# Work of the heads' stretch and after it is split in advance, kept in DRAM and loaded back; heads unrolled, sigmoids moved

## The reference, cut to what matters

```python
mod = silu_c @ ada_w[l] + ada_b[l]                  # shifts, scales, gates from c
h = _modulate(_rmsnorm(x, norm_w[l, 0]), sh1, sc1)
# layer 0, per head: one projection h @ w_in split in q, v, z_fwd, z_bwd, g; then
f = lb + (1.0 - lb) * jax.nn.sigmoid(z)             # k = (1 - lb) * sigmoid(-z)
S_t = diag(f_t) S_{t-1} + k_t v_t^T                 # both directions, o_t = S_t^T q_t
y = (rmsnorm(o_f + o_b) * g_norm * silu(g)) @ w_out
# layer 1: y = (gate_b * conv3(gate_c * xin)) @ w_out
x = x + g1 * _rmsnorm(y, norm_w[l, 1])
hf = _modulate(_rmsnorm(x, norm_w[l, 2]), sh2, sc2)
x = x + g2 * _rmsnorm((silu(gate) * up) @ ffn_w_out, norm_w[l, 3])
```

## Time and profile before

| | |
|---|---|
| time, median of 3 runs | 2781.76 us (2780.82 to 2784.55) |
| profiled execution: time, span | 2777.81 us, 2776.1 us |
| mean clock of PE granted over the span | 0.984 |
| busy: PE, PE's weight loads, DVE, ACT, POOL | 95%, 79%, 61%, 35%, 42% |
| transfers | 202.06 MB, mean 73 GB/s |
| chain that ended last | PE 75%, DVE 12%, issue 5%, ACT 3%, POOL 3%, DMA 1% |

### The profile page before, as it was taken

The page is one execution under the profiler, slowest core; times in us unless marked ns, Lnnn a source line. Parts: engine busy times, 40 slices in busy tenths (PEclk is TensorE's granted clock), DMA queues, the critical chain, the costliest instruction groups (busy, mean ns, idle before and its releaser), DMA issues.

```text
span 2776.1 us, 37193 instructions
## 1 busy us (share of the span) xinstructions
PE 2630.0 (95%) x12824; PEld 2183.6 (79%) x12824; DVE 1695.3 (61%) x2380; ACT 960.0 (35%) x1853; POOL 1165.1 (42%) x799
## 2 busy tenths in 40 slices
PE   7999999999969789999999989999897999999998
PEld 5788888888858668888888877888686888888886
DVE  6277668766875575656565565665438555554556
ACT  5334433443443642332223254111254233222323
POOL 2111111111160086665556542444517666556662
PEclk9999999999989999999999999999999999999999
DMA  6111221111110312122112132333311112111113
GB/s 244 61 46 39 62 62 46 40 61 54 39 53 13 133 39 75 62 82 77 60 60 69 60 137 91 118 117 114 129 61 38 61 46 68 53 45 45 60 46 144
DMA packets 57899, 202.06 MB, mean 73 GB/s; under 512 B 6832, under 2 KB 6832, under 8 KB 57776
## 3 DMA queue, kind: packets, MB, share of 16 engines
q1 hardware_dynamic: 57776, 200.41, 21.5%
HBM read 183.61 MB, written 16.78 MB: 72 GB/s over the span
## 4 chain that ended last, share of the span: by engine, by line
PE 75%; DVE 12%; issue 5%; ACT 3%; POOL 3%; DMA 1%; SPq 0%; DVEq 0%; POOLq 0%; ACTq 0%
PE psum L1027 16%; PE psum L1029 15%; PE psum L1028 15%; PE psum L1546 5%; PE psum L1548 5%; PE psum L1547 5%; PE psum L1222 2%; PE psum L1267 2%; PE psum L1269 2%; PE psum L1268 2%; DVE q_all L2431 1%; DVE c_set L2228 1%; PE psum L1236 1%; DVE q_all L2525 1%; DVE k_all L2424 1%
## 5 line engine op out<-in xcount | busy, mean ns | idle before, releaser
L1027 PE MATMUL psum<-x_hi,unit_hi 128*128 128x512 f32 x1232 | 486.9, 395 | 20.8 <-DVE x_lo L2228 12.8
L1028 PE MATMUL psum<-x_lo,unit_hi 128*128 128x512 f32 x1232 | 483.1, 392 | 0.0
L1029 PE MATMUL psum<-x_hi,unit_lo 128*128 128x512 f32 x1232 | 482.7, 392 | 0.0
L902 POOL TENSOR_TENSOR unit_sum<-ffn_raw 128x512 f32<-128x512 f32 x220 | 298.2, 1355 | 416.4 <-PE psum L1027 182.3
L2228 DVE TENSOR_TENSOR c_set<-c_set,psum 128x512 f32<-128x512 f32 x352 | 233.3, 685 | 345.8 <-PE psum L1029 179.7
L907 POOL TENSOR_TENSOR unit_lo<-unit_sum,unit_hi 128x512 fp32r<-128x512 f32 x220 | 286.8, 1312 | 185.1 <-ACT unit_hi L1660 184.9
L857 POOL TENSOR_TENSOR w_lo<-w_raw,w_hi 128x1024 fp32r<-128x1024 f32 x38 | 94.2, 2479 | 626.8 <-ACT w_hi L1660 626.8
L1027 PEld LDWEIGHTS psum<-x_hi,unit_hi 128*128 128x128 f32 x1232 | 233.3, 189 | 79.4 <-issue 22.6
L2228 DVE TENSOR_TENSOR y<-y,psum 128x512 f32<-128x512 f32 x288 | 193.7, 686 | 159.1 <-PE psum L1548 154.7
L1027 PE MATMUL psum<-h_hi,w_hi 128*128 128x512 f32 x640 | 270.7, 423 | 7.2 <-POOL w_lo L857 4.0
L1029 PEld LDWEIGHTS psum<-x_hi,unit_lo 128*128 128x128 f32 x1232 | 233.4, 189 | 49.4
(11 more groups left out here) (283 smaller groups left out, 5170.8 us busy)
## 6 DMA issues: line engine op xcount, KB each, us to landing
ffn_raw<-in_w_ffn_in SPq DMA_DIRECT2D x88, 512.0 KB, 3.7
ffn_raw<-in_w_ffn_out SPq DMA_DIRECT2D x44, 512.0 KB, 4.0
w_raw<-in_w_hgrn_in SPq DMA_DIRECT2D x40, 512.0 KB, 3.7
ada_raw<-in_ada SPq DMA_DIRECT2D x32, 512.0 KB, 4.3
conv_ada_raw<-in_ada SPq DMA_DIRECT2D x32, 512.0 KB, 4.0
conv_w_raw<-in_w_conv_in SPq DMA_DIRECT2D x24, 512.0 KB, 4.5
ada_first<-in_ada SPq DMA_DIRECT2D x4, 2048.0 KB, 14.8
kept<-xt SPq DMA_DIRECT2D x16, 512.0 KB, 2.8
```

Of the source, the lines that this page charges most:

```text
L902: pool.tensor_tensor(unit[2][:, :], one, other, op).then_inc(S["unit_summed"], 1)
L1027: begin = pe.matmul(out_ap, hi[:, a:b], rhs_hi, start=first, stop=False)
L1028: pe.matmul(out_ap, hi[:, a:b], rhs_lo, start=False, stop=False)
L1029: return begin, pe.matmul(out_ap, lo[:, a:b], rhs_hi, start=False, stop=last)
```

## The change

- New tensors in DRAM: `rows_kept`, `units_kept`, `mix_kept`. In head h (phase 1 to 7) there are three spots in ScalarE's, GpSimd's and SP's programs: A behind the last scores (ScalarE) and before the low part of panel 4 (GpSimd); B behind panel 4's high and low; C behind the last context evacuation (ScalarE), and directly behind B (GpSimd).
- Phases 1 to 3 split four rows each (two at A, two at C): rows 0 to 6 of the first out-projection, rows 3 to 7 of the convolution's. Phases 4 to 7 split the seven units of one FFN pair each (three at A with one sum, two at B and two at C with two sums each). From phase 2 on the mixed output of head phase - 2 is split at B. Each is stored in DRAM.
- They are loaded back where they are used, high and low parts together: rows 0 to 6 and six mixed outputs around the fill, 14 units for each FFN, five convolution rows. The work that made them there is gone. Row 7 and the mixed outputs of the last two heads are split late as before.
- The heads are unrolled on all engines. The sigmoids of a head run at the end of its projection head, before the last evacuation. `panel_high(1)` stands at the start of a head, `merge_level(3)` one evacuation earlier. In the last head ScalarE's order and PE's slots between the v transposes change.
- In the start panel 2 of head 0 has a place of its own and is split early; ScalarE builds four diagonal matrices, with `start_rows(1)` between them; PE does 12 small products first.

```diff
+SPLIT_HGRN, SPLIT_CONV = KB - 1, 3
+SPLIT_ROWS = [(0, r) for r in range(SPLIT_HGRN)] + [(1, r) for r in range(SPLIT_CONV, KB)]
+ROW_PHASES = len(SPLIT_ROWS) // 4
+SPOTS = A_SPOT, B_SPOT, C_SPOT = range(3)
+SPOT_UNITS = (0, 1, 2), (3, 4), (5, 6)
+SPLIT_KINDS = (M2, M4, M3, M5, M1, M7, M6)
+SPLIT_SUMS = tuple(kind for kind in SPLIT_KINDS if kind in SUMMED)
+SPLIT_MIXES = HEADS - 2
+
+
+def row_tasks(phase, spot):
+
+    first = 4 * (phase - 1) + {A_SPOT: 0, C_SPOT: 2}.get(spot, 4)
+    return [t for t in (first, first + 1) if spot != B_SPOT and 1 <= phase <= ROW_PHASES]
+
+
+def split_pair(phase):
+
+    return phase - 1 - ROW_PHASES if phase > ROW_PHASES else None
+
+
+def unit_tasks(phase, spot):
+
+    return [] if split_pair(phase) is None else list(SPOT_UNITS[spot])
...
+    rows_kept = nc.dram_tensor("rows_kept", (len(SPLIT_ROWS), P, 2 * D), F32, kind="Internal").ap()
+    units_kept = nc.dram_tensor("units_kept", (4 * PRODUCTS, P, D), F32, kind="Internal").ap()
+    mix_kept = nc.dram_tensor("mix_kept", (SPLIT_MIXES, 4, P, HALF), F32, kind="Internal").ap()
...
+            def stage_stores(phase, spot):
+
+                for t in row_tasks(phase, spot):
+                    sp.wait_ge(S["stage_low"], t + 1)
+                    sp.dma_start(rows_kept[t], as_f32(stage_row[t % 2][0][:, :, :])).then_inc(S[f"stage_stored{t % 2}"], 16)
+                m = split_mix(phase, spot)
+                if m is not None:
+                    sp.wait_ge(S["mix_split"], m + 1)
+                    for part, tile in enumerate((mix_hi, mix_lo[m % 2])):
+                        sp.dma_start(mix_kept[m, part::2].rearrange("h p t -> p h t"),
+                                     as_f32(tile[:, :]).rearrange("p (h t) -> p h t", h=2)).then_inc(S["mix_stored"], 16)
+                for j in unit_tasks(phase, spot):
+                    pair = split_pair(phase)
+                    sp.wait_ge(S["stage_low"], unit_number(pair, j))
+                    sp.dma_start(units_kept[PRODUCTS * pair + SPLIT_KINDS[j]], as_f32(stage_unit[j % 3][0][:, :, :])
+                                 ).then_inc(S[f"stage_stored{j % 3}"], 16)
...
+            for h in range(HEADS):
+                head_loads(h, h % 2)
...
+            def unit_load(f, k):
+
+                u, kind = FIRST_ORDER[k]
+                if k >= 4:
+                    sp.wait_ge(S["unit_started"], FFN_UNITS * f + k - 2)
+                sp.dma_start(as_f32(unit_parts[k % 4][0][:, :, :]), units_kept[PRODUCTS * (2 * f + u) + kind]
+                             ).then_inc(S[f"unit_loaded{k % 4}"], 16)
...
+            for m in range(SPLIT_MIXES):
+                for part in range(2):
+                    sp.dma_start(as_f32(mix_halves[0][part][0][:, m, :]), mix_kept[m, part]
+                                 ).then_inc(S[f"mix_loaded{m}"], 16)
+                if m == 3:
+                    row_load(4)
...
+            sp.wait_ge(S["gemm_full"], O_END)
+            for r in range(SPLIT_CONV, KB):
+                sp.dma_start(as_f32(conv_row_parts[r][0][:, :, :]), rows_kept[SPLIT_ROWS.index((1, r))]
+                             ).then_inc(S[f"conv_row_loaded{r}"], 16)
...
+            def stage_lows(phase, spot):
+
+                for t in row_tasks(phase, spot):
+                    _, hi, lo, raw = stage_row[t % 2]
+                    pool.wait_ge(S["stage_hi"], t + 1)
+                    pool.tensor_tensor(lo[:, :], raw[:, :], hi[:, :], ALU.subtract).then_inc(S["stage_low"], 1)
+                m = split_mix(phase, spot)
+                if m is not None:
+                    pool.wait_ge(S["mix_hi"], m + 1)
+                    pool.tensor_tensor(mix_lo[m % 2][:, :], mix[m % 2][:, :], mix_hi[:, :], ALU.subtract
                                        ).then_inc(S["mix_split"], 1)
-
-
-            def row_low(r):
-
-                pool.wait_ge(S["w_hi_done"], N_HGRN_OUT + r + 1)
-                pool.tensor_tensor(hgrn_rows[r][1][:, :], row_raws[r][:, :], hgrn_rows[r][0][:, :], ALU.subtract
-                                   ).then_inc(S["panel_split"], 1)
...
+            for n in range(4, N_HGRN_OUT):
+                h, i = n // HEAD_PANELS, n % HEAD_PANELS
+                if i == 4:
+                    stage_spot(h, A_SPOT)
+                panel_low(n, n % 2, ring[n % 2])
+                if i == 4:
+                    stage_spot(h, B_SPOT)
+                    stage_spot(h, C_SPOT)
...
+            for _ in range(12):
+                pe.matmul(bank(2, 0, P), ident[:, :], ident[:, :], start=True, stop=True)
...
+                    slots(6)
                     for part in range(3):
                         v_transposes(hs, part)
-                    slots(28)
+                        slots(1)
+                    slots(19)
                     for part in range(2):
...
+            def stage_highs(phase, spot):
+
+                for t in row_tasks(phase, spot):
+                    act.wait_ge(S[f"stage_loaded{t % 2}"], row_stored(t))
+                    copy(stage_row[t % 2][1], stage_row[t % 2][3][:, :], "stage_hi")
+                m = split_mix(phase, spot)
...
+                def sigmoids():
+
+                    act.wait_ge(S["gemm_evac"], hg * 10 + (4 + O_HEADS + 4))
+                    act.wait_ge(S["ctx_evac"], hg * 3 + 3)
+                    act.wait_ge(S["scan_full"], hg * SCAN_USES + U_TURN)
                     for d in (FWD, BWD):
                         copy(gates[d][:, :], z[d][:, :], "sigmoids", ACT.Sigmoid)
                     for d in (FWD, BWD):
                         copy(k[d][:, :], z[d][:, :], "sigmoids", ACT.Sigmoid, scale=-1.0)
...
+                    copy(first_third[0][:, :], w_raws[0][:, 0, :], "w_hi_done")
...
                 if hg is not None and hs is not None:
                     evacuate(0, 0, cols(z[FWD], 0, CTX))
-                    panel_high(1)
                     evacuate(0, 1, cols(z[FWD], 1, CTX))
                     evacuate_ctx(0, z[FWD][:, 0:CTX])
                     near_copies()
                     evacuate(1, 0, cols(z[BWD], 0, CTX))
                     panel_high(2)
+                    merge_level(3)
                     evacuate(1, 1, cols(z[BWD], 1, CTX))
                     evacuate_ctx(1, z[BWD][:, 0:CTX])
-                    merge_level(3)
                     merge_level(4)
...
                     if not last:
                         panel_high(5)
+                    sigmoids()
...
+                if inst == 0 and i < 4:
+                    return
```

More of the change, by code:

```diff
@@ L99, with split_mix, unit_number, sums_after @@
 PARTIALS = 16 * (FFN_GROUPS - 1)
+SPLIT_HGRN, SPLIT_CONV = KB - 1, 3
[13 more added lines that the diff above has]
+    return [] if split_pair(phase) is None else list(SPOT_UNITS[spot])
+def split_mix(phase, spot):
+    return phase - 2 if spot == B_SPOT and phase >= 2 else None
+def unit_number(pair, j):
+    return len(SPLIT_ROWS) + PRODUCTS * pair + j + 1
+def sums_after(pair, j):
+    return len(SPLIT_SUMS) * pair + sum(kind in SUMMED for kind in SPLIT_KINDS[:j + 1])
+def row_stored(t):
+    return 16 * (t // 2 + 1)
+def unit_stored(pair, j):
+    rows, each = (len(SPLIT_ROWS) // 2, len(SPLIT_ROWS) // 2, 0)[j % 3], (3, 2, 2)[j % 3]
+    return 16 * (rows + each * pair + j // 3 + 1)
 CTX_Q = 4
@@ L336, in build_trunk @@
     ffn_raw = at("ffn_raw", 176, [P, 3, D])
-    units = [unit_at(f"unit{i}", 188 + 4 * i) for i in range(4)]
+    unit_parts = [both_parts(f"unit{i}", 188 + 4 * i, HALF) for i in range(4)]
+    units = [(*parts[1:], at(f"unit{i}_sum", 190 + 4 * i, [P, HALF])) for i, parts in enumerate(unit_parts)]
     last_units = [[unit_at(f"last_unit{f}_{i}", (0, 32)[f] + 4 * i) for i in range(4)] for f in range(2)]
@@ L888, in _, with stage_sums @@
-            mix_low(0, (6,))
-            mix_low(1, range(KB - 1))
-            row_low(7)
+            panel_low(N_HEADS + 2, 0, first_third)
+            panel_low(N_HEADS + 3, 1, ring[1])
+            def stage_sums(phase, spot):
+                pair = split_pair(phase)
+                for j in unit_tasks(phase, spot):
+                    if SPLIT_KINDS[j] not in SUMMED:
+                        continue
+                    if pair == j == 0:
+                        pool.wait_ge(S["stage_stored1"], row_stored(len(SPLIT_ROWS) - 1))
+                    elif pair + j // 3 > 0:
+                        pool.wait_ge(S[f"stage_stored{j % 3}"], unit_stored(pair, j) - 16)
+                    for t in range(2):
+                        pool.wait_ge(S[f"stage_loaded{t}"], row_stored(len(SPLIT_ROWS) - 1) + 16 * (pair + 1))
+                    one, other, op = stage_terms(SPLIT_KINDS[j])
+                    pool.tensor_tensor(stage_unit[j % 3][3][:, :], one, other, op).then_inc(S["stage_sum"], 1)
@@ new lines, in stage_spot @@
+            def stage_spot(phase, spot):
+                stage_sums(phase, spot)
+                stage_lows(phase, spot)
+            for n in range(4, N_HGRN_OUT):
[6 more added lines that the diff above has]
```

(16 more changed lines are left out.)

378 lines of the change are left out of this document (206 added, 172 removed).

## The result

Median 2749.78 us (2748.13 to 2752.59, 4 runs) against 2781.62 us (2780.82 to 2784.55): a ratio of 0.9883, 95% interval 0.9871 to 0.9896, 31.8 us faster. Forecast were 2764, 17.9 faster: the sign and the range hold, the size was too small; the time lies at the lower edge of the forecast's own range (2750 to 2778), between it and rival (b), 2739. The profiled execution took 2749.15, its span 2747.4, so the two spans differ by 28.7; 3 of the 31.8 lie in how the profiled execution of before stood to its median.

The account below looks back on a forecast made before the run. PE was taken as the bound, busy 2630 of 2776 us, idle 146. Terms -2.5 -14 +48.6 -16 -11 -9 -14 = -17.9 gave 2764 from 2781.8; own range 2750 to 2778, 8-in-10 range 2708 to 2786.

Parts of the forecast that it names:

- rival (b): Heads: half of the collisions of VectorE with GpSimd's new work reach PE, 24.3 off, 2739 us; chance .15.
- the last scan: Last head: units ready from DRAM free VectorE from standing behind GpSimd, so near products start earlier, -16 us (-12 to -20).
- projection and FFN 0: First units load instead of being summed and split, so waits for unit lows go: -11 us (-8 to -15).
- conv rows: Convolution rows: five PE waits of 7.4 for GpSimd's lows and one half-clock stretch go, -9 us.
- FFN 1: Second FFN: PE's waits for x's low parts shrink as GpSimd's units are gone there, -14 us (-9 to -17).
- Start: First panels: own place for panel 2 saves 4.0 and clock 1.7, ScalarE's copies cost 3.2; net -2.5 us (-7 to +1).
- The heads' gains: Heads: earlier sigmoids -11, unrolling -3 for two loop turns, merge moved ahead 0; together -14 us.
- The heads' price: Heads: new GpSimd work delays VectorE's ada steps, hence states and PE, with clock loss; +48.6 us (0 to 105).
- knife edge: Heads, spot A: if the last ada step gets in before the panel's low, a unit phase costs 1.2, no clock.
- (a): Rival, heads: collisions don't reach PE, lows fall into other gaps or ada steps go first; -66.5, 2715 us; chance .2.
- (c): Rival, heads: GpSimd's new instructions make VectorE late everywhere; +50 at the bound, 2832 us, decides from 66.5; chance .1.
- (d): Rival, fill and conv rows: loads come late, 20 to 30 of 50 saved return as waits; 2784 to 2794, chance .1.

Follow-up runs that it names:

- the kernel with the lows behind: Against the changed kernel, GpSimd's lows of spot A stand behind the low of panel 4 instead of ahead of it: 2721.44 us, ratio 0.9794.

## Why the prediction was right, and where its size was off

**Sign and parts outside the heads.** By the marks each is within 1.5: the last scan (-16.5 of -16), projection and FFN 0 (-9.8 of -11), conv rows (-9.2 of -9, and 11.2 by the run that undid them alone), FFN 1 (-12.5 of -14; four of x's lows take 2.49 where they took 5.69, but a wait of 3.2 for them is left where the prediction's sign allowed 1.5). For all but the conv rows this is read from the two traces; no run undid these parts alone.

**The last scan: right by luck.** From VectorE's first q x gates to PE's near product the prediction had 17.8 and 1.3, 19.1. It took 23.9, with 6.6 of wait for ScalarE in it, which the prediction did not have. But q x gates started 5.0 after the ada sums where it had been 10.4, and the prediction had left that start where it was. Before, VectorE's steps ahead of it ran beside 9.35 of GpSimd's row lows (one gates step took 3.06 that takes 0.94 now), and the sigmoids came later. The two errors, 5.4 and 4.8, cancel.

**Start.** The sum (-3.3 of -2.5) is near, but its terms are not shown. Undoing ScalarE's diagonals, the row order and the small products together made the kernel 1.3 faster, within the runs' spread. By that they cost 1.3 and not 3.2, but a few us either way can't be told.

**The heads' gains: the term that was mis-sized.** Forecast -14. An undisturbed head, as measured in the kernel with the lows behind, is 90.12: seven of them are 631. Before took 655.2 from ada sums to ada sums, so the gain is -24. Two terms were too small. Unrolling was put at the two waits marked "issue", 3. Alone it measured 10.5, of which 9.0 lie between the ada sums in the two traces: 4.4 at the two turns and about 0.8 in each of the six distances in the loop, none in the seventh, outside it. At one turn the excess over the wait shown is a half-clock stretch, which the prediction missed when it took the clock in the heads as 1.00 throughout; what makes the bodies in the loop longer is not shown. The sigmoids were put at 11, the waits for near queries (7.4) and what follows them; they are worth 2.2 a head, 15 over seven heads, and 17 with the last scan. The merge was put at 0, and no run shows otherwise.

**The heads' price: size right, half of its mechanism wrong.** The changed heads take 678.8, less 631: +48, forecast +48.6. Heads 1 to 3 carry 20.5 of it; for them the prediction had 22.9 with the clock, by the collision of the ada steps with GpSimd's lows, and the run with the same work in another order shows that this is the cause: it takes away the long steps, the waits and the slow stretches together (5.9 of it went with the stores of A first too). For heads 4 to 7 the prediction had 25.6, by the same collision, and 27 came, but by another cause. The knife edge went the other way: the last ada step got in before the panel's low (in head 4 it was done 0.2 after the low began), and PE's waits for states there are at most 0.3. Only the sums beside the far levels are as forecast (1.1 a head for 1.25). The step that failed is the sentence "each store waits for a low finished long before the panel behind it is needed. 0". It asked when the store could be issued, and not who waits for its landing: the next unit in its place, behind it ScalarE's key copies, behind these PE. Two runs show its size: 14.5 went from heads 4 to 6 with the stores of A first, 8 from head 7 with those of B ahead of the row loads. That the two amounts agree is chance.

**Rivals.** By mechanism the collisions did what rival (b) says: about half of them reached PE, 20.5 in heads 1 to 3 and 4 to 5 from the sums, for the reason it names, the knife edge. Its time, 2739, was missed because two things that no rival had came on top: about 22 of waits for stores, and 10 more gain from unrolling and sigmoids. (a) did not come, as 20.5 of collision did reach PE. (c) did not come: 48, the clock included, reached PE, and it takes 66.5 and more. (d) shows in the fill only, 2.9 for mixed outputs.

**Its signs.** Waits for states did grow to 3.2 to 5.1, but in three heads and at the key x value products, not in all and at the BWD transposes. A head took 3 to 5 longer than before, as said. The ada steps took 2.6 to 2.9 in heads 1 to 3 and about 1.4 in head 4. Near in the last scan came 23.9 after its first q x gates, not 17.

**What would have been the better version.** With the orders changed, 2706.93 to 2708.2: ratio 0.973 to the kernel before where the change had 0.988. Of the price, 1.3 a head is left in heads 4 to 6, none in 1 to 3.

## What to carry to other kernels

Work that is moved under an idle engine's cover has to be placed against the other engine's instructions one by one: the same subtractions cost 20 us ahead of one panel's low and nothing behind it. A transfer that only frees a place is on the path as soon as an engine in order stands behind its reuse; ask of every store when it lands and what it is queued behind. And measure the gain of an unrolled loop by the distance between bodies, not by the wait shown where it turns.

## What the runs showed of the hardware

Stores of units and rows took longer to land than most loads in this kernel, by the medians. From the page of the changed kernel (KB each, median us to landing):

```profile
ffn_raw<-in_w_ffn_in SPq DMA_DIRECT2D x80, 512.0 KB, 3.5
...
units_kept<-stage_unit SPq DMA_DIRECT2D x28, 512.0 KB, 6.1
unit<-units_kept SPq DMA_DIRECT2D x28, 512.0 KB, 4.9
rows_kept<-stage_row SPq DMA_DIRECT2D x12, 1024.0 KB, 8.4
```

They are issued in clusters with ada and panel loads. The direction alone does not tell: in head 4 (470 to 500) a store of a mixed output landed after 2.9, and two panel loads of the same size after 7.3. What makes them late was not tried.

In the heads of the changed kernel the clock of PE fell at waits of 2.8 to 5.1, for 3.4 or 6.8 us, and the length of the wait does not tell which: at one of 3.2 it was 6.8, at one of 5.1 it was 3.4 and at another 6.8. Nor does the length tell whether it falls: in the kernel before it fell at the loop turn with a wait of 1.3 and not at the one with 1.8, and in the changed kernel's last scan not at one of 3.2.
